# Where the normalised activations of three FFNs start in SBUF, relative to the weights

## What is computed

```python
a = rmsnorm(h, norm2[i])
h = h + (jax.nn.silu(a @ w_gate[i]) * (a @ w_up[i])) @ w_down[i]
...
def swiglu(x, w_in, w_out):
    gate, up = jnp.split(x @ w_in, 2, axis=-1)
    return (jax.nn.silu(gate) * up) @ w_out
...
h = swiglu(rmsnorm_2(x, norm_ffn1_pre[l]), w_ffn1_in[l], w_ffn1_out[l])
...
h = swiglu(rmsnorm_2(x, norm_ffn2_pre[l]), w_ffn2_in[l], w_ffn2_out[l])
```

## Time and profile before

| | |
|---|---|
| time, median of 3 runs | 793.92 us (793.78 to 794.3) |
| profiled execution | 793.85 us, its span 792.0 us |
| TensorE (PE) busy | 781.6 us, 99% |
| VectorE (DVE) busy | 533.2 us, 67% |
| ScalarE (ACT) busy | 429.3 us, 54% |
| matmuls | 4710 |
| HBM read | 139.69 MB, 178 GB/s over the span |

### The profile page before, as it was taken

How to read it: one execution, slowest core, us unless ns; L and a number is a source line. 1 busy time by engine, 2 the same in 40 slices (tenths; PEclk the granted TensorE clock), 3 DMA queues, 4 the chain that set the end, 5 groups by cost and what they waited for, 6 DMA issues and landing times.

```text
span 792.0 us, 12209 instructions
## 1 busy us (share of the span) xinstructions
PE 781.6 (99%) x4710; PEld 687.9 (87%) x4710; DVE 533.2 (67%) x628; ACT 429.3 (54%) x565; POOL 28.3 (4%) x35
## 2 busy tenths in 40 slices
PE   9999999999999999999999999999999999999997
PEld 8989988888888888888888887999988888888885
DVE  7866657766666667866666566766977766666665
ACT  6556657544544448744544447565557654454444
POOL 0000000000000000000000000002520000000000
PEclk9999999999999999999999999999999999999999
DMA  9633433645555553665545554452444664555521
GB/s 335 235 110 112 143 115 128 245 166 205 191 183 209 175 196 110 238 224 199 198 176 209 183 188 159 142 204 108 161 165 162 221 223 166 205 192 183 208 106 54
DMA packets 20797, 141.16 MB, mean 178 GB/s; under 512 B 2448, under 2 KB 2704, under 8 KB 4384
## 3 DMA queue, kind: packets, MB, share of 16 engines
q1 hardware_dynamic: 20192, 138.65, 48.8%
q0 software_dynamic: 576, 2.10, 0.8%
HBM read 139.69 MB, written 1.05 MB: 178 GB/s over the span
## 4 chain that ended last, share of the span: by engine, by line
PE 94%; ACT 2%; DVE 2%; issue 1%; DMA 1%; SPq 0%; DVEq 0%; ACTq 0%
PE ps L1478 93%; ACT whi L695 1%; PE ps L1484 1%; DMA raw<-wstream 1%; DVE x L1227 0%; ACT squared L710 0%; DVE xa L1034 0%; PE ps L1707 0%; DVE wlo L1023 0%; PE ps L1677 0%; PE ps L1926 0%; DVE xg L1222 0%; DVEq L272 0%; ACT L928 0%; PE ps L1709 0%
## 5 line engine op out<-in xcount | busy, mean ns | idle before, releaser
L1478 PE MATMUL ps<-xa,whi 128*128 128x512 f32 (+2 forms) x1744 | 377.4, 347 | 0.0
L1023 DVE TENSOR_TENSOR wlo<-raw,whi 128x2048 fp32r<-128x2048 f32 x128 | 293.6, 2295 | 82.2 <-ACT whi L695 82.2
L1478 PEld LDWEIGHTS ps<-xa,whi 128*128 128x128 f32 x1744 | 299.6, 188 | 41.4 <-issue 2.1
L695 ACT ACTIVATE whi<-raw 128x2048 fp32r<-128x2048 f32 x128 | 244.2, 1909 | 6.9 <-PE ps L1478 6.8
L1478 PE MATMUL ps<-xa,wlo 128*128 128x256 f32 (+1 forms) x1376 | 219.8, 278 | 0.0
L1478 PEld LDWEIGHTS ps<-xa,wlo 128*128 128x128 f32 x1376 | 187.9, 188 | 2.8
L1478 PE MATMUL ps<-wlo,hhi 128*128 128x512 f32 x240 | 93.5, 390 | 0.0
L1478 PE MATMUL ps<-whi,hlo 128*128 128x512 f32 x240 | 93.5, 390 | 0.0
L1478 PE MATMUL ps<-whi,hhi 128*128 128x512 f32 x240 | 93.5, 390 | 0.0
L889 ACT ACTIVATE hhi<-arena 128x512 fp32r<-128x512 f32 x30 | 19.0, 633 | 88.4 <-PE ps L1478 81.9
L875 ACT ACTIVATE arena<-ps 128x512 f32<-128x512 f32 x33 | 19.7, 597 | 85.5 <-PE ps L1478 85.4
(11 more groups left out here) (221 smaller groups left out, 531.6 us busy)
## 6 DMA issues: line engine op xcount, KB each, us to landing
raw<-wstream SPq DMA_DIRECT2D x128, 1024.0 KB, 4.8
gain_row<-rows_in POOLq DMA_DIRECT2D x4, 512.0 KB, 3.9
x<-x_in SPq DMA_DIRECT2D x2, 512.0 KB, 4.0
raw<-wstream SPq DMA_DIRECT2D x2, 512.0 KB, 5.8
out<-x SPq DMA_DIRECT2D x4, 256.0 KB, 2.1
xg<-const_in SPq DMA_DIRECT2D x1, 912.0 KB, 11.8
small<-small_in SPq DMA_DIRECT2D x1, 152.0 KB, 6.1
arena<-meta_in SPq DMA_DIRECT2D x1, 64.0 KB, 4.5
```

Source lines behind the costliest of these rows:

```text
L695: nc.scalar.activation(whi[slot][:], raw[slot][:], ACT.Copy).then_inc(hi_ready, 1)
L1023: nc.vector.tensor_tensor(wlo[slot][:], raw[slot][:], whi[slot][:].bitcast(F32), ALU.subtract).then_inc(lo_ready, 1)
L1478: return nc.tensor.matmul(o, lhsT, rhs, start=start, stop=stop, skip_group_check=True)
```

## The change

One table. Norms 0, 1 and 3, those of the three FFNs, start 72, 76 and 84 floats into `xa` in place of 80, which is 288, 304 and 336 bytes on from the residue of the weights in place of 320. Norm 2, the mixer's, stays at 80 floats. The order of the instructions on each engine is the same in both kernels.

```diff
-XN_AT = ((80, SEQ),) * 4
+XN_AT = ((72, SEQ), (76, SEQ), (80, SEQ), (84, SEQ))
```

## The result

The changed kernel takes 802.44 us (median of 4 runs, 801.78 to 802.66) against 793.89 us for the kernel before (4 runs, 793.78 to 794.3): a ratio of 1.0107, 95% interval 1.0095 to 1.0119. It is slower by 8.5 us. The forecast was 796.5 us with a range up to 799.5: the sign was right, the size was not.

What follows compares the result with a forecast made beforehand. TensorE's matmul pace in the FFNs was taken as the bound. Writes 0, high products 0 and low products 2 x 1.3 us gave 2.6 us on 793.9, so 796.5 us, with an 8-in-10 range of 791.2 to 799.5.

Steps and rivals of the forecast that it cites:

- What bounds the kernel: TensorE in the FFNs: time is matmul count times pace, with no waits; TensorE is 94% of the chain.
- the writes at other addresses: 48 ScalarE and VectorE writes of the moved tile: taken as 0, at most 0.5 us.
- That the distance sets the pace: FFN matmuls: pace depends on how moving operand and loaded weights' addresses stand; high products 2.7 ns above down products.
- Low products: FFN 256-column products with the weights' low parts: 1.3 us lost in two of three FFNs, 2.6 us.
- the fast pattern: Low products in the looped FFN groups at 113.4 ns each, against 117.8 ns at the slow pace.
- High products: FFN 512-column products with the weights' high parts, 336 per FFN: taken as 0, between 0.9 us gain and 0.5 loss.
- The loss end: High products at 231.0 ns, 1.6 ns more each, 0.5 us per FFN.
- The sum: Whole kernel: 0 for writes, 0 for high products, 2 x 1.3 for low ones, 2.6 us more.
- (a): FFNs: nothing to measure, pace steps coarser than 16 or 32 bytes or FFNs cancelling; 793.9 us, chance 0.30.
- (b): FFN high products lose their extra 2.7 ns, 0.9 us per FFN; faster, 791.2 us, chance 0.26.
- (c): High and low products both at their loss ends in all FFNs; much slower, 799.3 us, chance 0.10.

Runs made afterwards that it cites:

- e1: Against the kernel before, a 32-byte pad ahead of all buffers, FFN distances staying at 320 bytes; 793.49 us against 793.68.
- e2: Against the kernel before, only the weights 32 bytes on, FFN activations at their old addresses, distance 288 in all three FFNs; 802.43 us against 793.68.
- e3: Against the kernel before, distances of 336, 288 and 304 bytes in the first, second and third FFN; 801.74 us against 793.68.
- e4: Against the kernel before, only the first FFN moved, to 288 bytes, the other two at 320; 797.37 us against 793.68.
- e12: Against the kernel before, only the down unit's stationary tiles, hhi and hlo, moved 64 bytes on; 802.60 us against 793.50.
- e5 to e7: Against the kernel before, FFN distances of 256, 384, 512; 64, 128, 192; and 448, 0, 832 bytes; 798.91, 798.00 and 796.59 us against 794.05.
- e11: Against the kernel before, FFN distances of 544, 48 and 80 bytes, the changed kernel's each shifted by 256; 802.27 us against 793.87.
- e8: Against the kernel before, FFN distances of 316, 324 and 328 bytes; 801.70 us against 794.05.
- e9: Against the kernel before, all FFNs at 288 bytes, high products loading only 32 and 64 columns in the first two; 799.94 us against 793.87.

## Why the prediction was right or wrong

**What bounds the kernel: right.** The time is TensorE's count times its pace. The rise is in the three unbroken runs of the chain; other engines kept their times, no wait came, and the writes at other addresses took 477 and 476 ns in the median where they had taken 476, as forecast.

**That the distance sets the pace: right, and now shown.** e1 and e2 separate it from the place itself, e3 and e4 from the FFN and the history between FFNs. The prediction had inferred it from the difference of the high products and the down products, which was thin evidence: in the kernel before, the down unit of the first FFN's written-out group, at the same distance 0, runs from 149.28 to 154.77 us, 228.8 ns a product, and that is as much as the second high run of the earlier trace rows. That the inference held is in part luck. The rule of the Trainium skill against which this stood ("TensorE: Matmul & The Clock Gate", section "Step-by-step: what each phase is for": loading weights takes no read bandwidth from the running matmul) does not hold to the nanosecond here: e12 moved the loaded tiles alone, and 24 products went from 227.1 ns each (5.45 us, from 182.16 to 187.61 in the earlier trace rows) to 233.3. Nor do the 16-byte lines that the Trainium skill gives ("SBUF — State Buffer", section "Door 1: The DMA port swizzle (why `[64,N]` ≈ `[32,N]`)") tell good places from bad ones: 304, a multiple of 16, costs 0.32 us a group and 316, which is none, 0.08.

**Low products: right in kind, too small.** I had taken 4.4 ns on 288 products for two FFNs of three, 2.6 us. All three lost the fast pattern, and two of them fell deeper than the slow pace that I knew: to 117.8, 118.4 and 120.0 ns. That is 288 x (4.4 + 5.0 + 6.6) = 4.6 us. "Which is as low as any 256-column product of this trace goes; they can't gain by anything seen" was right and was the strongest hint: the looped groups sat in the better of two patterns, so a step away could only lose. That the third FFN would keep the pattern had no row behind it.

**High products: the step that failed.** "I take 0: the ends lie on both sides, and 229.4 lies between them." They went from 229.4 on average to 233.4 in the first FFN, 233.1 in the second and 230.9 in the third: 336 x (4.0 + 3.7 + 1.5) = 3.1 us. The loss end was too near as well: 231.0 ns, from adding to a 512-column product the extra that a 272-column one had paid. The shape that has 512 columns was never seen at another distance than 0 and 320, and the extra of one shape did not carry over to another. That the ends lay on both sides of 229.4 was no reason for the middle: in the map 15 of 19 places have high products at 231 ns or more, and the highest first run, at 68, is 236.9, some 7 ns above the 230.0 of the kernel before.

**The sum.** 4.6 + 3.1 = 7.7 us of the 8.8 us of the span. Of the rest, 0.4 us had passed before the first FFN's run began (128.02 against 127.63), which is no more than such starts differ from run to run (127.28 in e1). The down units take a part: 24 products in 188.72 - 183.25 = 5.47 us in the first FFN against 5.45. The remainder lies in the written-out first groups, the products of 256 columns at their head and the stretches between the FFNs, and was not followed further.

**The rivals.** (a) was wrong: steps far finer than 16 bytes matter. (b) was half seen: distance 0 does give high products 226.9 ns, but takes more from the low ones (119.7), groups of 16.55 us. (c) came true and went past its price of 799.3 us, because both of its loss ends were too near; I had held it at 0.10 because an FFN's distances don't change from product to product. That protects from nothing: at the constant distance of 288 high products pay 7.1 ns over 226.7, more than the 4.3 of the projection.

## What to carry to other kernels

In a kernel like this one, with fp32r operands and a TensorE that runs without a gap, where the moving operand starts relative to the weight tiles was worth up to 2.8% of the time of a group (16.42 to 16.88 us), so measure it before and after any change of the allocation, even one that adds a small tensor or a pad in between: e12 moved two small buffers by 64 bytes and cost 9 us. Read it as start less start over a run of equal matmuls in the timeline, not from the durations or the busy share. If a kernel already shows the lowest pace that its shape has in the trace, expect most steps away to cost (here low products kept it at 2 of 18 other places, 16 and 192), and leave the loss open where the same shape was never seen elsewhere.

## What the runs showed of the hardware

With all weights at one residue, distances between a moving operand and a weight tile that agree in the remainder by 256 bytes gave the same pace: ten places in four classes (the nine of e5 to e7, and 320) and three more pairs (e11 and the changed kernel) agree within 0.01 us a group. Inside it 4 bytes can be the whole difference (64: 16.42 us, 68: 16.88). The place by itself, 32 bytes on for all operands (e1), changed nothing. Products of 512 columns were seen between 226.7 and 240.0 ns (e8, the second high run at 68: 3.84 us for 16), those of 256 columns between 113.3 and 120.0. At one and the same distance 256-column products hold either of two paces over hundreds of products, 113.4 or 118 ns, and moving only the stationary tiles of the down unit ahead of them (e12) switches it. The place of the tile that is loaded has a part in a product's pace: 227.1 ns became 233.3 (e12). The extra does not go in proportion to the length of the load: 231.3 ns with 32 and with 64 columns, 233.8 with 128 (e9).
